# Hybrid conv / gating / pooling trunk on eight cores: group matrices multiplied into the output weights on chip, convolution result stored time-major, value projection two tiles ahead

## The reference

```
h = rms_norm(x, norm1_g[l]);  z = h @ w_in[l]          # 1792 columns: 768 | 768 | 256
ya: y = a * sigmoid(gate)                              # a, gate = the first 768 columns
    y = causal depthwise conv of width 31 (y) + conv_b
    y = silu(layer_norm(y, ln_g, ln_b));  ya = y @ w_pw            # 384 x 384
yb: u, v = split(gelu(z));  v = layer_norm(v)
    s = einsum('hts,bnshd->bnthd', tril(w_s), v) + b_s;  yb = u * s   # chunks of 128
yc: p = trailing means over 2, 4, 8, 16 positions, minus the token
    yc = (p @ w_pool[g], 64 x 64 for each of 4 groups) * pool_scale
x = x + concat([ya, yb, yc]) @ w_out[l]                # 1024 x 1024
h = rms_norm(x, norm2_g[l]);  gate, up = split(h @ w_gate_up[l])   # 1024 x 5632
x = x + (silu(gate) * up) @ w_down[l]                  # 2816 x 1024
```

## Time and profile before

| | |
|---|---|
| time, median of 3 runs | 3058.99 us (3058.8 to 3324.05) |
| the profiled execution's own time | 3059.71 us |
| its span on the slowest core (core 0) | 3058.1 us |
| spans of the eight cores | 3019.6 to 3058.1 us |
| mean granted TensorE clock, core 0 / core 3 | 0.958 / 0.972 |
| busy: PE, PEld, DVE, ACT, POOL | 2844.7, 1451.3, 1207.3, 823.5, 177.4 us |
| PE's share of the chain that ended last | 84% |
| DMA | 148.44 MB, mean 49 GB/s |

### The profile page before, as it was taken

One profiled execution on the slowest core, in us unless ns is written; L12 is line 12 of the kernel. 1 busy time (PEld: TensorE's weight loads), 2 busy tenths in 40 slices (PEclk: granted clock), 3 DMA queues, 4 the chain that ended last, 5 costly groups with the idle time before them and its releaser, 6 DMA issues.

```text
span 3058.1 us, 44571 instructions; the slowest of 8 cores (3019.6 to 3058.1 us)
## 1 busy us (share of the span) xinstructions
PE 2844.7 (93%) x15632; PEld 1451.3 (47%) x15632; DVE 1207.3 (39%) x2108; ACT 823.5 (27%) x1356; POOL 177.4 (6%) x286
## 2 busy tenths in 40 slices
PE   5889999999997999999988889999999889999998
PEld 3554344444555444444465544444445544444444
DVE  2372422323554523223354633323335634223236
ACT  3544111010545220110255541010025442110102
POOL 2000000000001010000000001000000000000000
PEclk8887799999998999999998899999999899999999
DMA  8304062220131252221243034221003040222102
GB/s 188 53 1 70 3 94 38 42 32 14 25 53 23 48 83 35 42 36 31 74 151 76 8 63 65 52 42 35 14 15 60 17 69 4 39 41 43 29 21 111
DMA packets 123463, 148.44 MB, mean 49 GB/s; under 512 B 71664, under 2 KB 98416, under 8 KB 121200
## 3 DMA queue, kind: packets, MB, share of 16 engines
q0 software_dynamic: 37376, 100.80, 20.3%
q1 hardware_dynamic: 85872, 44.80, 5.5%
HBM read 219.12 MB, written 23.07 MB: 79 GB/s over the span
## 4 chain that ended last, share of the span: by engine, by line
PE 84%; DVE 6%; issue 4%; ACT 2%; DMA 2%; POOL 1%; SPq 1%; DVEq 0%; ACTq 0%; POOLq 0%
PE bank L332 78%; PE bank L350 2%; PE bank L726 2%; DVE bna L741 1%; ACT sqr L361 1%; PE bank L554 1%; DVE ybt L383 1%; DVE bnv L780 1%; DVE vn L383 1%; PE bank L720 1%; SPq L324 1%; DVE vg L383 1%; DMA yd<-ytok 1%; ACT silT L361 1%; POOL bna L746 1%
## 5 line engine op out<-in xcount | busy, mean ns | idle before, releaser
L332 PE MATMUL bank<-h2T,ring 128*128 128x512 bf16 x5632 | 1227.2, 380 | 0.0
L332 PEld LDWEIGHTS bank<-h2T,ring 128*128 128x128 bf16 x5632 | 551.5, 98 | 667.9 <-issue 22.6
L371 DVE TENSOR_TENSOR xT<-xT,bank 128x512 f32<-128x512 f32 x640 | 438.2, 687 | 506.2 <-PE bank L332 419.3
L332 PE MATMUL bank<-act,wd 128*128 128x512 bf16 x2816 | 618.1, 379 | 7.5 <-DVE r L377 3.7
L371 DVE TENSOR_TENSOR act<-tsil,bank 128x512 bf16<-128x512 f32 x352 | 242.2, 688 | 953.2 <-PE bank L332 945.4
L361 ACT ACTIVATE tsil<-bank 128x512 f32<-128x512 f32 x352 | 210.1, 597 | 1496.6 <-PE bank L332 1483.9
L332 PEld LDWEIGHTS bank<-act,wd 128*128 128x128 bf16 x2816 | 269.9, 98 | 323.4 <-issue 8.0
L361 ACT ACTIVATE sqr<-xT 128x512 bf16<-128x512 f32 x320 | 191.4, 624 | 207.3 <-PE bank L554 194.9
L332 PE MATMUL bank<-w_a_sb,xb 128*128 128x384 bf16 x1024 | 180.1, 336 | 12.9 <-DVE r L377 12.9
L332 PE MATMUL bank<-w_uv_sb,xb 128*128 128x384 bf16 x1024 | 184.0, 343 | 0.0
L332 PEld LDWEIGHTS bank<-w_uv_sb,xb 128*128 128x128 bf16 x1024 | 105.1, 103 | 78.2 <-issue 19.5
(11 more groups left out here) (123 smaller groups left out, 1762.0 us busy)
## 6 DMA issues: line engine op xcount, KB each, us to landing
ring<-w_gate_up POOLq DMA_DIRECT2D x88, 512.0 KB, 7.4
wd<-w_down POOLq DMA_DIRECT2D x12, 1536.0 KB, 12.1
xst<-x SPq DMA_DIRECT2D x24, 512.0 KB, 6.8
out<-osF SPq DMA_DIRECT2D x16, 512.0 KB, 4.3
w_a_sb<-w_a POOLq DMA_DIRECT2D x8, 768.0 KB, 16.3
w_uv_sb<-w_uv POOLq DMA_DIRECT2D x8, 768.0 KB, 27.0
yd<-ytok SPq DMA_DIRECT2D x16, 384.0 KB, 2.8
y<-yd SPq DMA_DIRECT2D x128, 48.0 KB, 2.9
```

Of the source, the lines that this page charges most:

```text
L332: ins = e.matmul(out, l, r, start=(first and i == 0), stop=(last and i == n - 1))
L371: return P.add(eng, lambda e, out=out, in0=in0, in1=in1, op=op: e.tensor_tensor(out=out, in0=in0, in1=in1, op=op), reads=reads, writes=writes)
```

## The change

1. **Weights multiplied on chip.** `PW` and `PM` are gone. For the first sequence (`s == 0`) of each layer, `fuse_a` computes `w_pw @ w_out[0:384]` (2 times 9 matmuls of 128 x 512, three ACT copies each, behind `Z(1)` and `Z(2)`) and `fuse_c` does the same for the pool matrices (2 times 2 matmuls, 2 copies, between the `lnt`; the scale goes into `wpl` by two DVE operations). `keep_wo` writes the products to DRAM (`wod`, bf16); the second sequence loads them (`load_wo`). The weights arrive transposed from the host. `WO` then multiplies `silT` and `yc` (now the transposed pool result itself, one ACT copy) directly, the `silT` terms last in each group.
2. **Time-major convolution result.** `xc` is two halves of 8 times by 384 channels, so that the LayerNorm's statistics, applications and transposes read channels side by side. The convolution's ACT copy now reads PSUM 16 elements apart and writes runs of 32. `lnt` goes by channel tile (`ct`, three of them) instead of by time: 16 transposes into four PSUM banks at once (`next_quad`), then four Silu activations, each reading PSUM 128 elements apart (`(t b)` read as `b t`), and it needs the whole LayerNorm (`("lna", s, l, 3)`). `xc` lies over toep's first four blocks, so the copies of blocks 0 to 3 are held until block 3's matmuls are recorded.
3. **Value projection two tiles ahead.** `V(1)` stands inside `conv`, behind block 5; `V(j+2)` stands behind `SP(j)`. `TR` now comes before `PT`, and each `conv` block ticks twice.
4. **Buffers.** The output weights lie in `woA` (over `toep`, so their load waits for the convolution) and `woB`; the ring's slots are six pieces; the first down weights (`load_wd(l, 0)`) are loaded from `after()`, eight gate/up pairs into FFN, since they share space with `woA`.

```diff
+    def next_quad():
+        r = bank_rr[0] % 8
+        qi = 1 if 0 < r <= 4 else 0
+        bank_rr[0] = 4 * qi + 4
...
-    def conv():
+    def conv(mid):
+        def ev(bk, bb, b):
+            act_op(xcv[:, :, :, 32 * b:32 * b + 32], bk[:].rearrange("p (c h t) -> p h t c", h=2, t=8), AF.Copy,
+                   [bb], xc_b(b))
...
-            act_op(xc[:, 32 * b:32 * b + 32, :].rearrange("p c t -> p (c t)"), bk[:], AF.Copy, [bb], [xc_b(b)])
-            tick()
+            held.append((bk, bb, b))
+            if b >= 3:
+                for x in held:
+                    ev(*x)
+                held = []
+            tick(2)
+            if b == 5:
+                mid()
...
-    def lnt(s, l, tq):
-        need_lo(("lna", s, l, tq))
-        for ct in range(3):
-            bk, bb = next_bank()
...
+    def lnt(s, l, ct):
+        need_lo(("lna", s, l, 3))
+        qk, qb = next_quad()
+        for tq in range(4):
+            transposes([(qk[:, (4 * tq + ti) * 128:(4 * tq + ti + 1) * 128],
+                         xct(4 * tq + ti)[:, ct * 128:(ct + 1) * 128], identF[:]) for ti in range(4)],
...
+        for j in range(NJ):
+            act_op(silT[:, ct, j * NT:(j + 1) * NT].rearrange("p (b t) -> p b t", t=TB),
+                   qk[:].rearrange("p (t b) -> p b t", t=TB)[:, 32 * j:32 * j + 32, :], AF.Silu, qb + [bPV],
...
+    def fuse_a(h):
...
+        for ci in range(3):
+            bk, bb = next_bank()
+            mm(bk[:], [(w_pw[:, mk, ci * 128:(ci + 1) * 128], woA[:, mk, hs]) for mk in range(3)],
...
+            act_op(woA[:, ci, hs], bk[:], AF.Copy, [bb], [wo_b(0, h)])
...
-            pairs = [(wo[:, i, nc_], y[:, i, :]) for i in range(3)]
-            pairs += [(wo[:, 3 + i, nc_], ybT[j][:, i, :]) for i in range(3)]
-            pairs += [(wo[:, 6 + i, nc_], yc[j][:, i, :]) for i in range(2)]
+            pairs = [(woA[:, 5, nc_], ybT[j][:, 0, :])] + [(woB[:, i, nc_], ybT[j][:, 1 + i, :]) for i in range(2)]
+            pairs += [(woA[:, 3 + i, nc_], yc[j][:, i, :]) for i in range(2)]
+            pairs += [(woA[:, i, nc_], silT[:, i, jt]) for i in range(3)]
...
+            conv(lambda s=s, l=l: V(s, l, 1))
+            load_wo(s, l)
...
-                need(("vn", s, l, j))
-                if j + 1 < NJ:
-                    V(s, l, j + 1)
...
                 SP(s, l, j)
+                if j + 2 < NJ:
+                    V(s, l, j + 2)
                 Z(s, l, j)
+                if s == 0 and j in (1, 2):
+                    fuse_a(j - 1)
+                TR(s, l, j)
                 if j > 0:
                     PT(s, l, j - 1)
-                TR(s, l, j)
-                if j > 0:
-                    PM(s, l, j - 1)
```

More of the change, by code:

```diff
@@ L211, in build_program @@
     out_d = nc.dram_tensor("out", [nseq, S, D], F32, kind="ExternalOutput").ap()
+    wod = [nc.dram_tensor("wod%d" % i, [128, 5, D], BF16, kind="Internal").ap() for i in range(L)]
     yd = [nc.dram_tensor("yd%d" % i, [S, DA], BF16, kind="Internal").ap() for i in range(2)]
@@ L279, in build_program @@
     toep = AT("toep", 61440, [128, NG, ND, NI, TB], BF16)
-    xc = AT("xc", 61440, [128, DA, TB], F32)
-    ring = [AT("ring%d" % i, 61440 + 8192 * i, [128, 2, 8, 256], BF16) for i in range(NRING)]
-    wd = AT("wd", 86016, [128, 6, D], BF16)
+    xc = AT("xc", 0, [128, 2, 15360], F32)
+    RGO = [[61440, 65536], [69632, 86016], [90112, 94208]]
+    ring = [[AT("ring%d_%d" % (i, h), RGO[i][h], [128, 8, 256], BF16) for h in range(2)] for i in range(NRING)]
+    wd0 = AT("wd0", 73728, [128, 6, D], BF16)
+    wd1 = AT("wd1", 77824, [128, 4, D], BF16)
     zh = [AT("zh%d" % i, 86016 + 4096 * i, [128, 4, DC], BF16) for i in range(2)]
@@ L298, in build_program @@
     sgB = AT("sgB", 129216, [128, 2, DB], F32)
-    ya = [AT("ya%d" % i, 110784 + 3072 * i, [128, 3, NT], BF16) for i in range(2)]
     cb32 = AT("cb32", 132288, [32, DA], BF16)
+    wpf = AT("wpf", 133056, [128, 2, 128], F32)
     cbf = AT("cbf", 124608, [32, DA], F32)
@@ L309, in build_program @@
     osF = [AT("osF%d" % i, 28672 + 4096 * i, [128, D], F32) for i in range(8)]
-    banks = [nc.alloc_psum_tensor("bank%d" % i, [128, 512], F32) for i in range(8)]
+    quads = [nc.alloc_psum_tensor("quad%d" % i, [128, 2048], F32) for i in range(2)]
+    banks = [quads[i // 4][:, 512 * (i % 4):512 * (i % 4) + 512] for i in range(8)]
     bank_rr = [0]
@@ L321, in next_bank @@
         raise AssertionError("all PSUM banks are held")
+    def next_quad():
+        r = bank_rr[0] % 8
+        qi = 1 if 0 < r <= 4 else 0
+        bank_rr[0] = 4 * qi + 4
+        bs = [B("bank", 4 * qi + i) for i in range(4)]
+        for b_ in bs:
+            assert b_.w is None or len(b_.r) > 0
+        return quads[qi], bs
     def dma(q, out, in_, reads=(), writes=(), final=False):
@@ L479, in load_wd, with wd_t @@
+    def wd_t(ci):
+        return wd1 if ci == len(CHUNKS) - 1 else wd0
     def load_wd(l, ci):
         f0, nf = CHUNKS[ci]
[L481 removed]
+        dma("gpsimd", wd_t(ci)[:, 0:nf, :], w_down_d[l, :, f0:f0 + nf, :], [], [bwd(ci)])
     def bwd(ci):
[L484 removed]
+        return wd_t(ci).b()
     x_dma(0, 0)
@@ L987, in FFN @@
                 bk, bb = next_bank()
-                mm(bk[:], [(wd[:, fi, n * 128:(n + 1) * 128], act[:, fi, jc(j)]) for fi in range(nf)],
+                mm(bk[:], [(wd_t(ci)[:, fi, n * 128:(n + 1) * 128], act[:, fi, jc(j)]) for fi in range(nf)],
                    [act_b(fi, j) for fi in range(nf)] + [bwd(ci)], [bb])
@@ L1097, in build_program, with after @@
                 nxt = 0
-            def after(nxt=nxt):
+            def after(s=s, l=l, nxt=nxt):
+                load_wd(l, 0)
                 if nxt is not None:
                     load_w_a(nxt)
-                    load_w_rest(nxt)
+                    load_w_rest(s if nxt else s + 1, nxt)
             FFN(s, l, after)
```

134 lines of the change are left out of this document (73 added, 61 removed).

## The result

The changed kernel took 3006.99 us (median of 4) where the kernel before took 3062.3 beside it: a ratio of 0.9832, 95% interval 0.9803 to 0.986. It is faster by 1.7%, less than the 3.0% forecast and less than the 2% that the forecast took as the least a measurement tells from no change, and the time lies 4 us above the range. Later, on another chip, the same kernel took 2982.08 against 3052.18, ratio 0.9751 (0.9692 to 0.9811); that time lies within the range.

A forecast was written before the change was run, and what follows sets the result against it. The prediction took DVE's queue to bound the mixing loop up to tile 2's ybt, ACT lnt and PE WO. Its terms, 18.6 - 5.4 + 7.0 + 4.6 - 1.5, gave 23.3 us a pass, 92 in all: 2967 us, range 2940 to 3003.

The forecast's parts named there:

- WO, 4.6 us gained: Output projection: PW's matmuls leave it, saving 4.6 us a pass.
- The loop, 64.3 us: Mixing loop: less DVE work ahead of tile 2's ybt shortens it from 82.9 to 64.3 us a pass, gaining 18.6.
- the forecast's own boundary: Mixing loop counted as ending with Z(3), the stage from the loop to WO starting there.
- The fused products are free, and only just: First sequence's mixing loop: 5.2 us of fuse_a matmuls cost nothing while DVE finishes later than PE's 64.0 us.
- Cheaper reads: Mixing loop: contiguous reads cut DVE's 12 statistics by 2.7 us and nine applications by 2.5 us a pass.
- Convolution, 5.4 us more: Convolution: V(1)'s PE work adds 5.4 us a pass; holding the first four copies costs nothing.
- Loop to WO, 7.0 us gained: lnt and PW stage between mixing loop and WO: shortens from 21.8 to 14.8 us a pass.
- The slow start of WO, 1.5 us: Start of WO: a lower clock after PE idles in lnt gives back 1.5 us a pass.
- Costed at nothing: Later loading of down weights in FFN and of output weights costs nothing; uncovered down weights would cost 12 us a pass.
- The first rival: ACT's strided PSUM reads cost time: 2986 us, or 2998 if copies also delay the loop; chance 0.17.
- The clock rival: Denser matmuls bring a slow-clock spell into three more passes on the slowest core: 3036 us; chance 0.08.
- without even the one spell: 2944: Whole kernel: 2944 us if core 0's first-pass clock spell, 23 us, is also absent.

The follow-up runs named there:

- e2: Changed kernel with PW(2) and PW(3), their copies and ticks put back in WO as work nobody reads; ratio 0.9751 to the kernel before.
- e3: Changed kernel with only three single ticks where PW(2) and PW(3) each stood, without their matmuls; ratio 0.9696 to the kernel before.
- e1: Changed kernel with WO ticking 4 closures behind each group instead of 5; mean of four executions 2935.8 us, 0.962 of the kernel before.
- e4: Changed kernel with the old loop order: V(j+1) at the loop's head, none in the convolution, PT ahead of TR; ratio 0.988 to the kernel before.
- e8: e1 with the second sequence also multiplying the weights on chip instead of loading the products; 2935 and 2941 us, ratio 0.9628 to the kernel before.
- e5: Changed kernel with the convolution's result stored channel by channel, 32 bytes between elements; ratio 0.9806 to the kernel before.
- the changed kernel (again): The changed kernel, unedited, run on another chip without a spell at 0.81; 2980 to 2984 us.

## Why the prediction missed

The direction and most of the mechanism were right. Of the miss of 40 us in time, some 15 belong to the kernel and 25 to the clock. Without either one the time would have been within the range: the spell adds 25 us, and WO is 27 us over its forecast.

- **WO, 4.6 us gained: wrong.** This is the step of the sum that failed. It subtracted 18 matmuls from WO and kept everything else, although my own reading had the closures recorded at ticks, and PW(2) and PW(3) had three each. WO went from 73.6 to 75.7, 6.7 us a pass over the forecast's 69, 27 in four. The matmuls were priced about right (4.3 us by e2 and e3); the waits that their ticks had kept away, 5.4 us by e3, were missing from the sum. e3 shows it (three bare ticks give 5.4 back) and e1 (no batch of five: 65.0).
- **The loop, 64.3 us: 63.9 by the forecast's own boundary, an average of 61.6 and 66.2, and in half of the passes by another limit.** Tile 2's `ybt` was forecast to end 49.5 us into the loop. In the third pass it ends at 1666.0, 48.1 in; in the second at 900.5, 49.7 in:

```profile
897.74 2.79 DVE L396 SCALAR_TENSOR_TENSOR ybt<-quad,pv,ug 128x384 bf16<-128x384 f32 x4 [1.62 <-PE quad L345]
```

  In the second pass, one of those with `fuse_a`, DVE has waited for PE: its queue no longer sets that point. In the third DVE doesn't wait there and PE waits 1.8 us for its `ybt`: there the forecast's mechanism holds, with a number 1.4 us too high. That the two kinds of pass average to 64 is luck. The third part of the change, which e4 undoes as a whole, is worth 12.5 us of loop and costs 4.9 of convolution.
- **"The fused products are free, and only just": wrong.** The text took the later of two limits, 64.0 us for PE's own work and 64.3 for DVE. PE's own work is less, 59.5 us of the 65.8 in the second pass, at a granted clock of 0.97 where the earlier trace rows had 0.90 for the loop; but PE's new waits for `zl` (6.2 us) come on top of work, not beside it. The loop takes 67.1 us in the fused passes and 62.5 in the others, and e8 moves 3.9 us with the products, against the 5.2 of the text. With e5, where 4.9 us more of DVE's work lengthen the loop by 5.0, this shows that neither engine hides the other's work any more.
- **Cheaper reads:** statistics 544 ns (559 forecast), applications 470 (360 forecast, 637 before). The 360 came from an operation that writes bf16, scaled by its length; it was 0.110 x 9 = 1.0 us a pass too low. e5, with steps of 32 bytes in place of the 64 of before, prices both together at 5.0 us of loop, 17 us in all, where the sum had 5.2.
- **Convolution, 5.4 us more:** 4.9 by the table. No wait behind the four held copies.
- **Loop to WO, 7.0 us gained:** 4.4 by the forecast's boundary (21.8 to 17.4); on core 7's second pass 15.7 against 14.8. The stage is 2.6 us longer than forecast on average, more in the second sequence. On core 7's third pass the first Silu starts 5.1 us behind the loop (4.4 forecast) and the two rounds take 5.0 and 5.9 us (4.8); in the second of them ACT waits 2.2 us for transposes that take 2.9 us in place of 2.0, at a granted clock of 0.90 in the stage. No run tested this.
- **The slow start of WO, 1.5 us:** as means over all cores and passes, the grant in WO's first 5 us is 1.00 before, 0.83 in the changed kernel (again) and 0.88 to 0.90 in e1. So there is a slow start, of 0.17 x 5 = 0.8 us. The changed kernel loses as much again later in WO, the kernel before 1.0 us, e1 none: that half belongs to the waits inside WO.
- **Costed at nothing:** no wait for `wd` appears in FFN, whose matmuls are as before. ACT's strided reads of PSUM took 602 ns (599 before) and `silT` 777 (796 before). The first rival is out. It needn't have been one: the prediction has `ya<-bank` of the earlier trace rows "read side by side and written apart", and it is the other way round. The code rearranges `(t b)` to `b t` in PSUM and writes `ya` contiguously, so that row already was an ACT read of PSUM 128 bytes apart, at 596 ns against the 599 of the contiguous `xc<-bank`.
- **The clock rival** is the one that happened in part. It was priced at three more spells on the slowest core; one spell on cores 4 and 5, 36 us between cores 4 and 7 and some 25 us in the kernel's time, did it, because it did not hit the slowest core of an even field but made one. The kernel before had such a spell too and paid less for it: 3059 us against 3052 elsewhere. So "without even the one spell: 2944" was too low as well, since the other cores were close behind core 0; the changed kernel took 2982 where no trace has a spell. The Trainium skill, "TensorE: Matmul & The Clock Gate", Part 1, describes a limiter that holds a whole die at 13/16 of the clock as long as three of its cores run dense matmuls. The trace agrees in the level (0.81) and not in the rest: it held two cores for 160 us while the other two of the die stood at 0.98 and FFN ran dense on all eight.

The sum of the terms, measured less forecast: WO +6.7, loop to WO +2.6, loop -0.4, convolution -0.5, and -1.5 for the slow start, which the forecast gave back apart and which is already in WO. Less 0.8 us because the mean pass before was 196.2 and not 195.4 us long, the gain is some 6 us a pass smaller than forecast: 24 in four, of which 22 are seen.

The best kernel is e1. One number, the batch at which deferred work is recorded, gave 46 us, two thirds of what the whole change gave.

## What to carry to other kernels

Where deferred work is recorded at ticks, a removed operation takes its ticks along: list which closures fall into one batch before and behind the edit, above all a producer on one engine and its consumer on another. Work that stands between two stages may be hiding a wait; price its removal by the waits of the neighbouring stage, not by its duration. And where a second engine's queue is shortened until it ties with PE's own work, nothing added to either engine is free any more (e8 on PE, e5 on DVE).

## What the hardware showed unasked

- ACT's *write* of f32 at 32-byte steps into SBUF costs nearly as much again as the whole copy: 1140 ns against 602 for 512 elements, with the same strided read of PSUM in both (e5). Strided reads of PSUM by ACT, 64, 128 and 512 bytes apart, cost nothing that the rows show.
- In SBUF a step of 32 bytes is no better than one of 64: statistics 837 and 788 ns against 544, applications 629 and 637 against 470. The Trainium skill, "Advanced Engine Details and Errata", SBUF Cachelines, has lines of 16 bytes of which at least two hits are needed; that both steps pay agrees with it, and the runs have no step of 8 bytes to test the other side.
- The spells at 0.81 came in pairs of cores (0 and 1, 2 and 3, 4 and 5), some 140 to 160 us long, on one chip, and in none of the traces taken on the three others.
